# Five attention steps change places with their neighbours in the written orders of layers 1 and 2

## The reference

```python
k_all = concat([kc, kl]); v_all = concat([vc, vl])
y_attn = attend(ql, k_all, v_all) * silu(a_g)          # 8 heads of 64, softmax over keys
oc, s = gla_scan(qcg, kcg, vcg, gfc, zeros)            # decayed linear attention, chunked
ol, _ = gla_scan(qlg, klg, vlg, gfl, s)                # and the same on the flipped sequence
y_gla = rms_norm(ol + flip(ol_b)) * silu(g_g)
y_sgu = s_u * mix(layer_norm(s_v)) * silu(s_g)
out = (sigmoid(m_a) * (y_attn @ w_br_attn) + sigmoid(m_g) * (y_gla @ w_br_gla)
       + sigmoid(m_s) * (y_sgu @ w_br_sgu)) @ w_out
x = layer_norm(alpha * x + gate * out)
```

## Time and profile before

| | |
|---|---|
| median of the runs | 1485.64 us (1485.33 to 1485.95) |
| profiled execution, time and span | 1484.53 us, 1482.7 us |
| PE busy | 1457.2 us (98%) |
| DVE, ACT, POOL busy | 851.5, 450.3, 307.3 us |
| PE's share of the chain that ended last | 91% |

### The profile page before, as it was taken

One profiled execution on the slowest core, in us unless ns is written; L12 is line 12 of the kernel. 1 busy time (PEld: TensorE's weight loads), 2 busy tenths in 40 slices (PEclk: granted clock), 3 DMA queues, 4 the chain that ended last, 5 costly groups with the idle time before them and its releaser, 6 DMA issues.

```text
span 1482.7 us, 21691 instructions
## 1 busy us (share of the span) xinstructions
PE 1457.2 (98%) x8912; PEld 1187.5 (80%) x8912; DVE 851.5 (57%) x1687; ACT 450.3 (30%) x905; POOL 307.3 (21%) x308
## 2 busy tenths in 40 slices
PE   7999999999999999999999999899999999999998
PEld 2677777657788888855978988798889889888887
DVE  1376666654533357622766753548688354777935
ACT  1232355324122111122335440143423213333321
POOL 0233302210566451231110403110100031010012
PEclk9999999999999999999999999999999999999999
DMA  9632222201322213431332353434332243333231
GB/s 385 256 144 114 114 114 114 114 21 37 148 88 94 95 66 124 158 114 57 115 114 114 115 210 131 160 114 170 114 115 86 104 166 139 145 114 115 89 139 43
DMA packets 17959, 184.40 MB, mean 124 GB/s; under 512 B 2370, under 2 KB 2882, under 8 KB 5316
## 3 DMA queue, kind: packets, MB, share of 16 engines
q1 hardware_dynamic: 17860, 183.01, 32.3%
HBM read 181.95 MB, written 1.05 MB: 123 GB/s over the span
## 4 chain that ended last, share of the span: by engine, by line
PE 91%; DVE 3%; ACT 3%; issue 1%; DMA 1%; POOL 1%; SPq 0%; DVEq 0%; POOLq 0%; ACTq 0%
PE ps L910 87%; PE ps L965 4%; DVE arena L2042 1%; DVE arena L2036 1%; DMA arena<-in_rp 1%; POOL arena L2852 0%; POOL arena L2856 0%; ACT arena L1560 0%; ACT L1996 0%; ACT L1994 0%; DMA arena<-in_wf 0%; DVE arena L2258 0%; DVE arena L2457 0%; ACT arena L1590 0%; ACT arena L1994 0%
## 5 line engine op out<-in xcount | busy, mean ns | idle before, releaser
L910 PE MATMUL ps<-arena 128*128 128x256 f32 (+7 forms) x8420 | 1409.5, 350 | 11.7 <-DMA arena<-in_wf 6.7
L910 PEld LDWEIGHTS ps<-arena 128*128 128x128 f32 (+4 forms) x8420 | 1134.4, 179 | 255.8 <-issue 127.3
L2852 POOL TENSOR_TENSOR arena<-arena 128x256 f32<-128x256 f32 (+6 forms) x252 | 276.2, 1118 | 849.3 <-DVE arena L2042 299.2
L2036 DVE TENSOR_TENSOR arena<-arena 128x512 f32<-128x512 f32 (+14 forms) x348 | 299.4, 887 | 169.5 <-ACT arena L1560 96.8
L1560 ACT ACTIVATE arena<-ps 128x512 f32<-128x512 f32 (+2 forms) x355 | 166.3, 489 | 568.6 <-PE ps L910 512.6
L2042 DVE SCALAR_TENSOR_TENSOR arena<-arena 128x256 f32<-128x256 f32 (+4 forms) x496 | 238.9, 534 | 106.2 <-ACT arena L1590 24.3
L2036 DVE TENSOR_TENSOR arena<-ps,arena 128x512 f32<-128x512 f32 (+16 forms) x157 | 64.5, 433 | 89.1 <-PE ps L910 82.7
L2042 DVE SCALAR_TENSOR_TENSOR arena<-arena,ps 128x256 f32<-128x256 f32 (+2 forms) x103 | 43.9, 439 | 81.8 <-PE ps L910 61.1
L965 PEld LDWEIGHTS ps<-arena 128*128 128x128 f32 x488 | 56.1, 142 | 33.1 <-issue 15.3
L965 PE MATMUL ps<-arena 128*128 128x128 f32 x488 | 73.4, 280 | 7.9 <-ACT arena L1560 5.4
L2039 DVE TENSOR_SCALAR arena<-arena 128x256 f32<-128x256 f32 (+10 forms) x179 | 62.1, 382 | 13.7 <-POOL arena L2852 10.8
(11 more groups left out here) (96 smaller groups left out, 299.3 us busy)
## 6 DMA issues: line engine op xcount, KB each, us to landing
arena<-in_wf SPq DMA_DIRECT2D x68, 2048.0 KB, 7.7
arena<-in_wf SPq DMA_DIRECT2D x22, 1024.0 KB, 6.2
arena<-in_first SPq DMA_DIRECT2D x3, 1024.0 KB, 20.1
arena<-in_wf SPq DMA_DIRECT2D x2, 1152.0 KB, 11.7
arena<-in_xin SPq DMA_DIRECT2D x4, 512.0 KB, 5.0
arena<-in_rp SPq DMA_DIRECT2D x2, 1024.0 KB, 9.9
arena<-in_consts SPq DMA_DIRECT2D x1, 1410.0 KB, 22.6
arena<-in_pa SPq DMA_DIRECT2D x2, 532.0 KB
```

Source lines behind the costliest of these rows:

```text
L910: return e.matmul(o, l, r, start=start, stop=stop, skip_group_check=True)
L2036: return e.tensor_tensor(o, x, y, op)
L2852: return e.tensor_tensor(o, x, y, op)
```

## The change

Two strings are edited; nothing else.

```diff
 ORDER_A = [
-    "dddadaaddadddddadaadddaggadaggadgagdgddaagggaaggdgagadadgddagagdaagadgagadgagagdagaaggaadaaggaadgagggaadggaagdaa"
-    "dagdaagagdaaagddadagggaagggadggadgadaggaadgaadagagadagaagaggdadaadgadadaggdaagdgagadaadadaddagg",
-    "aaddddddaddgadadadgagdddgaddggdgddddgaddggaddgadaddggdgaaddggadaadgdgdaaddagddgdgadgagagdgadgaadadgadgadagggdaaa"
-    "ddgdggdgadgdgadagddgadgggagagdgdggadggaggadgagggadgagdadgaddadgggagggg"]
+    "dddadaaddadddddadaadddaggadaggaddgaggddaagggaaggdgagadadgddagagdaagadgagadgagagdagaaggaadaaggaadgagggaadggaagdaa"
+    "dagdaagdagaaagddadagggaagggadggadgadagaagdgaadagagadagaagaggdadaadgadadaggdaagdgagadaadadaddagg",
+    "aaddddddaddgadadadgagdddgaddggdgddddgaddggaddgadaddggdgaaddggadaadgdgdaaddagddgdgaddgagaggadgaadadgadgadagggdaaa"
+    "ddgdggdgadgdagdagddgadgggagagdgdggadggaggadgagggadgagdadgaddadgggagggg"]
```

## The result

The changed kernel takes 1498.12 us (1497.29 to 1498.94, two runs) where the kernel before takes 1485.64: a ratio of 1.0084 [1.0068, 1.0101], 12.5 us more. The forecast was 1494.5, its range ended at 1498.0. Sign and class came as written, and the time lies just above the range.

The account below looks back on a forecast made before the run. PE was taken to bound the kernel. Terms for places 1 to 5, 3.3 + 3.1 + 0.6 + 2.4 - 0.5 = +8.9 us, added to 1485.64 gave 1494.5 us, range 1488.5 to 1498.0.

Parts of the forecast that it names:

- Sign and class: Whole kernel: 0.6% slower, in the class within 2% of the kernel before, chance 0.98.
- What bounds it: PE, busy 1457.2 of 1482.7 us with 25.5 us idle: each new wait of it is paid in full.
- Place 1: gv.6 and gv.7 ahead of the transposes of d0: PE waits for KD before those of d1, +3.3 us.
- faster: Rival, whole kernel: old waits go and none comes, 2.4 us won, 1483.2 us; chance 0.05.
- Place 2: es.5 and ef.6 ahead of T7.1: on DVE, weight additions come ahead of KD of d1, +3.1 us.
- Places 3 and 5: T10.0 ahead of l2 waits for DVE, +0.6 us; T4.1 fills the wait before transposes of d0, -0.5 us.
- Place 4: Second layer: bt waits for DVE's copy of row, and its ACT copy delays E2 and S3, +2.4 us.
- The clock: Rival: PE's granted clock falls after the new wait in place 1, costing 1.7 us, 1496.2 us; chance 0.21.
- a second fall: Case of the clock rival, no place named: PE's clock falls twice, 1497.9 us; no chance of its own.
- place 2 costs little: Rival: in place 2 the weights land sooner relative to PE, without the 3.1 us, 1490.4 to 1491.4 us; chance 0.09.
- nothing: Rival: PE's list changes only where other work takes the time anyway, 1485.6 us; chance 0.05.

Follow-up runs that it names:

- place 1 alone: Only gv.6 and gv.7 moved ahead of the transposes of d0, against the kernel before: 1490.71 us, ratio 1.0035.
- place 4 alone: Only bt moved ahead of l4, S3 and l5, against the kernel before: 1490.02 us, ratio 1.0033.
- the whole change with only place 1 filled: Eight idle PE products added to the whole change, ahead of the wait for KD of d1: 1497.43 us, ratio 1.0074 against the kernel before.

## Why the prediction was wrong: what held, and what failed

**What bounds it** held. PE does all it did, and each new wait is paid in full: nothing behind place 5 gave any of it back.

**Place 1** was forecast at +3.3. From the products ahead to the transposes of d1 it took 121.16 - 102.65 = 18.51 us, where it took 117.23 - 102.08 = 15.15: +3.36. The wait itself is 3.62 against a forecast of 3.6. One slip in it: the lower bound and the rival "faster" counted 0.9 us to be won. The wait of 0.58 goes, but `gv.6` then waits for ACT's copy of `gv.1`, 0.31 us with place 1 alone, so only about 0.3 were there. It moved no number that was taken.

**Place 2** (+3.1) measured +2.65 (from `T0.0` to the transposes of d1 124.00 us, before 121.35). DVE's additions and KD behind them in the changed kernel:

```profile
255.27 3.09 DVE L2036 TENSOR_TENSOR arena<-arena 128x1024 f32<-128x1024 f32 x3 [2.96 <-DMA arena<-in_wf]
```

All three take 3.09 us. The forecast had 2.78 for the additions and 0.69 for KD, 3.47: 0.38 of the missing 0.45 is this row, the rest the load, which came a little sooner (255.27 - 134.42 = 120.85 us behind `T0.0`, before 249.77 - 128.76 = 121.01).

**Places 3 and 5** (+0.6, -0.5) measured +0.70 (40.33 us from the transposes of d1 to T10.1, before 39.63) and -0.43.

**Place 4** (+2.4) measured 0.87 + 1.47 = 2.34 us of waits, in the two places and with the two releasers that were named.

The waits sum to 3.36 + 2.65 + 0.70 + 2.34 - 0.43 = 8.62 us, against the forecast's 8.9.

**The clock** is the step that failed, twice: the sum put it at nothing in both places. Behind place 1 its fall was named, priced at 1.7 us and then given a chance of 0.21, because 3.6 us were "a little less" than the 3.80 of the earlier trace rows. It fell in each of the three profiles that hold this wait (the changed kernel twice, place 1 alone) and in none of the four in which the wait was filled or covered. Its size was right: 13.26 - 11.53 = 1.73 us. In place 4 no fall was expected at all, because "all shorter waits went by at full clock" and these waits "come in pieces"; a second fall was priced (1497.9 us) and set the range's end, but it had no place, and it had one stretch, not two. That was the wrong reading. The clock fell in all four profiles with these two waits (the changed kernel twice, place 4 alone, the whole change with only place 1 filled) and in none without them, and cost 5.46 - 2.34 = 3.1 us in the changed kernel (PE's busy time in that piece rose by 3.15). Why it falls there is open. Between the two waits PE did `bt`, products of 2 rows (the 2 of `2*128`), and l4, of 64 rows (the row of 1.77 us holds both), and behind them S3 and l5, again of 64 rows. These products alone do not bring the clock down, since the kernel before and the one with `bt` behind E2 do the same ones at 1.00. Nor do short waits beside products of 64 rows always: the kernel before has two of them in layer 1, in a part that ran at full clock:

```profile
100.87 0.70 PE L910 MATMUL ps<-arena 64*128 64x256 f32 x4 [0.69 <-ACT arena L1560]
102.08 7.17 PE L910 MATMUL ps<-arena 128*128 128x256 f32 x32 [0.50 <-DMA arena<-in_wf]
```

No run here changes the work around a wait and leaves the wait as it is.

With both falls the sum is 8.62 + 1.73 + 3.12 = 13.47 us, the four pieces of the windows above (3.12 is what the third has beyond its waits). The likeliest time would have been 1485.6 + 8.9 + 1.7 + 3.1 = 1499.3 us, between the two medians of the changed kernel, 1498.12 and 1501.05.

The Trainium skill, page "TensorE: Matmul & The Clock Gate", section "HAM oscillation — how this bites in real kernels", warns of long gaps between bursts. In place 1 the traces agree with it (3.62 us, three of three). In place 4 the clock fell with no wait longer than 1.47 us, once behind 0.87 us alone, which a rule on the length of a gap does not give; the measurement decides.

The rivals "place 2 costs little", "faster" and "nothing" fall with the rows of the waits. The prediction's last sentence said where to look if PE's idle time were 34 us and the time above 1495: at the granted clock after place 1. That was the right place, and half of the answer.

## What to carry to other kernels

Where an order by hand moves a product forward, ask first what it covered where it stood: in place 1 two products hid the chain that makes the next keys, and without them PE waited 3.62 us. Then look for what it now stands in front of on the engines that work on its step: here a copy of 0.6 us ahead of a softmax on ACT, and additions that wait for a load ahead of a 0.69 us product on DVE, cost PE more than the waits that the move filled. A new wait of TensorE costs its length and may cost the clock behind it, at 1.7 us per stretch here; put that fall into the sum, and do not leave it out because the wait is short. How to tell beforehand which short wait brings it is not shown here. Products that nobody needs, put into a wait, kept the clock up behind it in all four kernels that have them.

## What was not expected of the hardware

- In place 4, with two waits of 0.87 and 1.35 to 1.47 us, the clock fell to 0.50 in four of four profiles; in place 2, with one of 1.81 to 1.99 us, in one of five.
- The clock comes back after 3.41 us or after two such stretches, 6.83: 3.40 us with place 4 alone and 6.83 in the whole change, and at the end of layer 2 3.41 and 6.80 in two executions of the same kernel. Every profile here has the fall at the end of layer 2, that of the kernel before too.
- In all four kernels with idle products a load at the end of layer 2, 190 to 840 us behind them, landed some 1.0 us sooner. Whether the products or the program around them do that is open.
